# The router product of two tiles at once in three fp32r passes, in the output projection of an encoder layer

## The reference

```python
o = concat([rms_norm(o_a, gqa_out_norm_g), rms_norm(o_b, mla_out_norm_g)])   # heads' outputs, 1024 wide
h = h + o @ w_out                                                            # 1024 x 1024
u = rms_norm(h, norm_ffn_g)
lg = u @ w_rg + b_rg          # 4 groups
le = u @ w_re + b_re          # 32 experts
# the best group, and the best two of its 8 experts, then silu(x @ w_gate) * (x @ w_up) @ w_down
```

## Time and profile before

| what | value |
|---|---|
| median of 3 runs | 3897.84 us (3897.72 to 3899.2) |
| the profiled execution | 3894.24 us, its span 3892.3 us |
| mean granted clock of TensorE | 0.961 |
| the output projection in the trace | 2650.0 to 3033.0 us |
| in it, 2790 to 2990 us | PE busy 200.0, DVE 88.1, ACT 71.2 us |
| router products (L1688) | 384 passes, 192 products, 24 tiles |

### The profile page before, as it was taken

The page is one execution under the profiler, slowest core; times in us unless marked ns, Lnnn a source line. Parts: engine busy times, 40 slices in busy tenths (PEclk is TensorE's granted clock), DMA queues, the critical chain, the costliest instruction groups (busy, mean ns, idle before and its releaser), DMA issues. The chain is left out here.

```text
span 3892.3 us, 53957 instructions
## 1 busy us (share of the span) xinstructions
PE 3599.2 (92%) x17079; PEld 2878.0 (74%) x17079; DVE 2776.8 (71%) x4984; ACT 2341.2 (60%) x4266; POOL 1221.9 (31%) x1105
## 2 busy tenths in 40 slices
PE   7999969999999999999999999998999389999991
PEld 7999946666766676788888888876888367777770
DVE  5666668888988898889888988864444655555553
ACT  4444406777777777777777777785333055555554
POOL 0000001011110111488888888891000023333320
PEclk9999969999999999999999999998999799999995
DMA  5465681332133213320332133003433088888877
GB/s 178 164 228 174 199 197 63 65 65 44 27 63 65 44 27 65 63 55 16 65 64 44 27 64 65 7 8 114 146 135 124 23 275 261 269 261 258 257 210 281
DMA packets 315271, 462.88 MB, mean 119 GB/s; under 512 B 120641, under 2 KB 251997, under 8 KB 303869
## 3 DMA queue, kind: packets, MB, share of 16 engines
q1 hardware_dynamic: 256468, 368.47, 32.3%
q0 software_dynamic: 19152, 69.74, 7.0%
q10 hardware_dynamic: 39456, 22.29, 1.9%
HBM read 313.38 MB, written 147.54 MB: 118 GB/s over the span
## 5 line engine op out<-in xcount | busy, mean ns | idle before, releaser
L997 POOL TENSOR_TENSOR b_p_lo<-b_prob,b_p_hi 128x512 fp32r<-128x512 f32 x704 | 916.9, 1313 | 782.5 <-ACT b_prob L1041 778.1
L1040 ACT ACTIVATE b_p_hi<-b_psS 128x512 fp32r<-128x512 f32 (+1 forms) x1376 | 824.4, 599 | 531.1 <-PE b_psS L1232 512.8
L1232 PE MATMUL b_psS<-b_q,b_k 96*128 96x512 f32 (+3 forms) x3440 | 1067.6, 408 | 25.3 <-DMA b_q<-b_nmxT 23.5
L1041 ACT ACTIVATE b_prob<-b_psS 128x512 f32<-128x512 f32 (+1 forms) x1376 | 818.2, 595 | 0.0
L1232 PEld LDWEIGHTS b_psS<-b_q,b_k 96*128 96x128 f32 (+3 forms) x3440 | 599.8, 184 | 189.4 <-DMA b_q<-b_nmxT 26.4
L1142 DVE TENSOR_REDUCE b_mx_s<-b_psM 128x1 f32<-128x412 f32 (+1 forms) x1228 | 679.4, 580 | 68.6 <-PE b_psM L1283 58.2
L1283 PE MATMUL b_psM<-b_k,b_q 96*128 96x412 f32 (+7 forms) x1596 | 558.4, 355 | 29.5 <-DMA b_q<-QGL 21.8
L1273 PE MATMUL b_psO<-b_p_lo,b_v 128*65 128x512 f32 (+1 forms) x1280 | 508.3, 397 | 0.4 <-POOL b_p_lo L997 0.4
L1110 DVE TENSOR_TENSOR b_p_lo<-b_prob,b_p_hi 128x512 fp32r<-128x512 f32 x576 | 418.8, 733 | 66.0 <-ACT b_prob L1041 58.1
L1125 DVE TENSOR_TENSOR b_acc<-b_acc,b_prob 128x512 f32<-128x512 f32 (+1 forms) x592 | 409.3, 691 | 45.6 <-ACT b_prob L1041 29.6
L1283 PEld LDWEIGHTS b_psM<-b_k,b_q 96*128 96x128 f32 (+1 forms) x1596 | 305.0, 191 | 139.0 <-DVE b_mx_s L1142 32.6
(11 more groups left out here) (256 smaller groups left out, 5758.4 us busy)
## 6 DMA issues: line engine op xcount, KB each, us to landing
e_w_gu<-w_gate SPq DMA_DIRECT2D x34, 1024.0 KB, 6.2
e_w_gu<-w_up SPq DMA_DIRECT2D x34, 1024.0 KB, 12.4
e_w_dn<-w_down SPq DMA_DIRECT2D x34, 1024.0 KB, 14.0
a_x_raw<-xallT SPq DMA_DIRECT2D x25, 512.0 KB, 5.1
a_x<-xall SPq DMA_DIRECT2D x25, 512.0 KB, 4.2
c_o<-O SPq DMA_DIRECT2D x24, 512.0 KB, 4.9
c_x<-xall SPq DMA_DIRECT2D x24, 512.0 KB, 3.2
H<-c_h SPq DMA_DIRECT2D x24, 512.0 KB, 2.6
```

Source lines behind the costliest of these rows:

```text
L997: nc.gpsimd.tensor_tensor(p_lo[:, slot, :], prob[:, slot, :], p_hi[:, slot, :].bitcast(F32), ALU.subtract).then_inc(lo_ready, 1)
L1040: nc.scalar.activation(p_hi[0:kn, slot, :], psS[0:kn, j % 2, :], ACT.Exp)
L1041: nc.scalar.activation(prob[0:kn, slot, :], psS[0:kn, j % 2, :], ACT.Exp).then_inc(p_ready, 1)
L1232: m = nc.tensor.matmul(psS[0:kn, j % 2, :], kk[s][0:r, k], qq[s][0:r, q], start=n == 0, stop=n == len(passes) - 1)
```

## The change

The router product is made for two tiles at a time and with fp32r operands. `w_rr` holds the two parts of `w_r` side by side, 36 columns of the rounded weights and 36 of the rest; ACT and DVE make it once at the start. `uT` becomes `uT_hi` and `uT_lo`, each of two tiles: ACT rounds `psU` (`uT_round`), and DVE subtracts (`uT_rest`) where it had copied. `route(j)` multiplies `uT_hi` by all 72 columns and `uT_lo` by the first 36, 16 products of 256 columns, into 72 rows of `psR`. `lg_out(j)` adds the bias (0 in the second 36 rows) for both tiles. `l_turn(j)` multiplies by `fold`, two unit matrices one above the other, so that the rows are turned and added at once. Both stand in the odd tile only, l_turn before its y product and route behind it. y, the loads and the stores stay as they are.

```diff
--- before.py
+++ after.py
@@ -1394,7 +1394,9 @@
         w_hi = sb("w_hi", [P, KC, D], F32R)
         w_lo = sb("w_lo", [P, KC, D], F32R)
         w_r = sb("w_r", [P, KC, NR])
-        b_r = sb("b_r", [NR, 1])
+        w_rr = sb("w_rr", [P, KC, 2 * NR], F32R)
+        fold = sb("fold", [P, NR])
+        b_r = sb("b_r", [2 * NR, 1])
         g_ffn = sb("g_ffn", [P, D])
         eps = sb("eps", [P, 1])
         o = sb("o", [P, 2, D])
@@ -1412,13 +1414,14 @@
         hstd = sb("hstd", [P, 2])
         hr = sb("hr", [P, 2])
         u2 = sb("u2", [P, 2, D])
-        uT = sb("uT", [P, KC, P])
-        lg = sb("lg", [P, P])
+        uT_hi = sb("uT_hi", [P, KC, 2 * P], F32R)
+        uT_lo = sb("uT_lo", [P, KC, 2 * P], F32R)
+        lg = sb("lg", [P, 2 * P])
 
         psA = ps("psA", [P, 2, 512])
         psY = ps("psY", [P, 2, 512])
         psU = ps("psU", [P, 2, 512])
-        psR = ps("psR", [NR, 512])
+        psR = ps("psR", [2 * NR, 512])
         psL = ps("psL", [P, 512])
 
         small_loaded = sem("small_loaded")
@@ -1429,7 +1432,8 @@
         ostd_ready, orr_ready, os_ready = sem("ostd_ready"), sem("orr_ready"), sem("os_ready")
         oT_psum, oT_ready, hi_ready, lo_ready = sem("oT_psum"), sem("oT_ready"), sem("hi_ready"), sem("lo_ready")
         y_psum, h2_ready, hstd_ready = sem("y_psum"), sem("h2_ready"), sem("hstd_ready")
-        u2_ready, uT_psum, uT_ready = sem("u2_ready"), sem("uT_psum"), sem("uT_ready")
+        u2_ready, uT_psum, uT_rounded, uT_ready = sem("u2_ready"), sem("uT_psum"), sem("uT_rounded"), sem("uT_ready")
+        w_r_rounded, w_r_ready = sem("w_r_rounded"), sem("w_r_ready")
         r_psum, lg_ready, l_psum, l_ready = sem("r_psum"), sem("lg_ready"), sem("l_psum"), sem("l_ready")
         h_stored = [sem("h_stored0"), sem("h_stored1")]
 
@@ -1526,6 +1530,11 @@
                 nc.scalar.activation(hstd[:, s:s + 1], hss[:, s:s + 1], ACT.Sqrt, scale=1.0 / D,
                                      bias=eps[:, 0:1]).then_inc(hstd_ready, 1)
 
+            def uT_round(T, s):
+                act.wait_ge(uT_psum, T + 1)
+                nc.scalar.activation(uT_hi[:, :, s * P:s * P + P], psU[:, :, :].rearrange("p b (c n) -> p (b c) n", n=P),
+                                     ACT.Copy).then_inc(uT_rounded, 1)
+
             def w_round(c):
                 nc.scalar.activation(w_hi[:, c, :], w_raw[:, c, :], ACT.Copy).then_inc(w_hi_ready, 1)
 
@@ -1538,10 +1547,14 @@
             oT_rounded(0, 0)
             for c in range(2, KC):
                 w_round(c)
+            act.wait_ge(small_loaded, 16 * 3)
+            nc.scalar.activation(w_rr[:, :, 0:NR], w_r[:, :, :], ACT.Copy).then_inc(w_r_rounded, 1)
 
             def body(T, j, s):
                 if at_least(T, 1):
                     h_stats(T - 1, 1 - s)
+                if at_least(T, 2):
+                    uT_round(T - 2, s)
                 if below(T, N - 1):
                     oT_rounded(T + 1, 1 - s)
                 if below(T, N - 2):
@@ -1549,6 +1562,8 @@
 
             over_tiles(act, body)
             h_stats(N - 1, 1)
+            uT_round(N - 2, 0)
+            uT_round(N - 1, 1)
 
         @block.vector
         def _(dve):
@@ -1584,17 +1599,19 @@
                 nc.vector.scalar_tensor_tensor(u2[:, s, :], h2[:, s, :], hr[:, s:s + 1], g_ffn[:, :],
                                                ALU.mult, ALU.mult).then_inc(u2_ready, 1)
 
-            def uT_out(T):
-                dve.wait_ge(uT_psum, T + 1)
-                nc.vector.tensor_copy(uT[:, :, :], psU[:, :, :].rearrange("p b (c n) -> p (b c) n", n=P)).then_inc(uT_ready, 1)
-
-            def lg_out(T):
-                dve.wait_ge(r_psum, T + 1)
-                nc.vector.tensor_scalar(lg[0:NR, :], psR[:, 0:P], b_r[:, 0:1], None, ALU.add).then_inc(lg_ready, 1)
-
-            def l_out(T):
-                dve.wait_ge(l_psum, T + 1)
-                nc.vector.tensor_copy(logits[:, bass.ds(T * NR, NR)], psL[:, 0:NR]).then_inc(l_ready, 1)
+            def uT_rest(T, s):
+                dve.wait_ge(uT_rounded, T + 1)
+                part = slice(s * P, s * P + P)
+                nc.vector.tensor_tensor(uT_lo[:, :, part], psU[:, :, :].rearrange("p b (c n) -> p (b c) n", n=P),
+                                        uT_hi[:, :, part].bitcast(F32), ALU.subtract).then_inc(uT_ready, 1)
+
+            def lg_out(j):
+                dve.wait_ge(r_psum, j + 1)
+                nc.vector.tensor_scalar(lg[0:2 * NR, :], psR[:, 0:2 * P], b_r[:, 0:1], None, ALU.add).then_inc(lg_ready, 1)
+
+            def l_out(j):
+                dve.wait_ge(l_psum, j + 1)
+                nc.vector.tensor_copy(logits[:, bass.ds(j * 2 * NR, 2 * NR)], psL[:, 0:2 * NR]).then_inc(l_ready, 1)
 
             def w_rest(c):
                 dve.wait_ge(w_hi_ready, c + 1)
@@ -1613,12 +1630,16 @@
             oT_rest(0, 0)
             for c in range(2, KC):
                 w_rest(c)
+            nc.vector.tensor_tensor(fold[:, :], ident[:, 0:NR], ident[:, NR:2 * NR], ALU.add)
+            dve.wait_ge(w_r_rounded, 1)
+            nc.vector.tensor_tensor(w_rr[:, :, NR:2 * NR], w_r[:, :, :], w_rr[:, :, 0:NR].bitcast(F32), ALU.subtract)
+            dve.drain().then_inc(w_r_ready, 1)
 
             def body(T, j, s):
                 if at_least(T, 1):
                     h_out(T - 1, j - 1 if s == 0 else j, 1 - s)
                 if at_least(T, 2):
-                    uT_out(T - 2)
+                    uT_rest(T - 2, s)
                 if below(T, N - 1):
                     oT_out(T + 1)
                 if at_least(T, 1):
@@ -1627,23 +1648,21 @@
                     oT_rest(T + 1, 1 - s)
                 if below(T, N - 2):
                     o_recip(T + 2, s)
-                if at_least(T, 4):
-                    l_out(T - 4)
-                if at_least(T, 3):
-                    lg_out(T - 3)
+                if at_least(j, 2):
+                    if s == 0:
+                        lg_out(j - 2)
+                    else:
+                        l_out(j - 2)
 
             over_tiles(dve, body)
             h_out(N - 1, N // 2 - 1, 1)
-            uT_out(N - 2)
+            uT_rest(N - 2, 0)
             u_out(N - 1, 1)
-            l_out(N - 4)
-            lg_out(N - 3)
-            uT_out(N - 1)
-            l_out(N - 3)
-            lg_out(N - 2)
-            l_out(N - 2)
-            lg_out(N - 1)
-            l_out(N - 1)
+            lg_out(N // 2 - 2)
+            uT_rest(N - 1, 1)
+            l_out(N // 2 - 2)
+            lg_out(N // 2 - 1)
+            l_out(N // 2 - 1)
 
         @block.tensor
         def _(pe):
@@ -1678,46 +1697,46 @@
                     i = nc.tensor.transpose(psU[:, c // 4, (c % 4) * P:(c % 4) * P + P], uv[:, c, :], ident[:, :])
                 i.then_inc(uT_psum, 1)
 
-            def route(T):
-                if isinstance(T, int) and T == 0:
-                    pe.wait_ge(small_loaded, 16 * 3)
-                pe.wait_ge(uT_ready, T + 1)
-                if at_least(T, 1):
-                    pe.wait_ge(lg_ready, T)
-                for c in range(KC):
-                    i = nc.tensor.matmul(psR[:, 0:P], w_r[:, c, :], uT[:, c, :], start=c == 0, stop=c == KC - 1)
-                i.then_inc(r_psum, 1)
-
-            def l_turn(T):
-                pe.wait_ge(lg_ready, T + 1)
-                if at_least(T, 1):
-                    pe.wait_ge(l_ready, T)
-                nc.tensor.transpose(psL[:, 0:P], lg[:, :], ident[:, :]).then_inc(l_psum, 1)
+            def route(j):
+                if isinstance(j, int) and j == 0:
+                    pe.wait_ge(w_r_ready, 1)
+                pe.wait_ge(uT_ready, 2 * j + 2)
+                if at_least(j, 1):
+                    pe.wait_ge(lg_ready, j)
+                for c in range(KC - 1):
+                    nc.tensor.matmul(psR[:, 0:2 * P], w_rr[:, c, :], uT_hi[:, c, :], start=c == 0, stop=False)
+                    nc.tensor.matmul(psR[0:NR, 0:2 * P], w_rr[:, c, 0:NR], uT_lo[:, c, :], start=False, stop=False)
+                nc.tensor.matmul(psR[0:NR, 0:2 * P], w_rr[:, KC - 1, 0:NR], uT_lo[:, KC - 1, :], start=False, stop=False)
+                nc.tensor.matmul(psR[:, 0:2 * P], w_rr[:, KC - 1, :], uT_hi[:, KC - 1, :], start=False, stop=True).then_inc(r_psum, 1)
+
+            def l_turn(j):
+                pe.wait_ge(lg_ready, j + 1)
+                if at_least(j, 1):
+                    pe.wait_ge(l_ready, j)
+                for s in range(2):
+                    i = nc.tensor.matmul(psL[:, s * NR:s * NR + NR], lg[:, s * P:s * P + P], fold[:, :], start=True, stop=True)
+                i.then_inc(l_psum, 1)
 
             pe.wait_ge(mix_loaded, 16 * len(MIX_PARTS))
             o_turn(0, 0, first=True)
             o_turn(1, 1)
 
             def body(T, j, s):
-                if at_least(T, 4):
-                    l_turn(T - 4)
+                if s == 1 and at_least(j, 2):
+                    l_turn(j - 2)
                 y_of(T, s)
```

(16 more changed lines are left out.)

## The result

| what | before | after |
|---|---|---|
| median of 5 runs | 3898.94 us (3897.72 to 3902.82) | 3873.73 us (four of them 3865.32 to 3876.16) |
| after / before | | 0.9929, 95% interval 0.9916 to 0.9942 |
| the profiled execution | 3894.24 us, span 3892.3 | 3871.39 us, span 3869.5 |
| the output projection, first load to the first instruction of the routing | 383.3 us | 360.9 us |

The fifth run after took 5263.24 us at a mean granted clock of 0.628; the ratio leaves it out, the median counts it, and without it the median would be 3872.56.

What follows compares the result with a forecast made beforehand. TensorE's own instructions were taken to bound the output projection. Gains 17.5 + 2.2 + 1.35, less 0.75 and 0.3, made 20.0 us: 3877.8 us from the 3897.84 median, range 3874 to 3886.

Steps and rivals of the forecast that it cites:

- rival A: Output projection: the gain comes as worked out from what leaves TensorE's queue, 17 to 23 us; chance 73%.
- The u transposes: TensorE, each tile: transposes of u take 0.89 us after the change, against 0.99 behind the old router product.
- the o transposes: TensorE, each tile: transposes of o with the way to the next y take 0.81 us.
- the turn: TensorE, once per two tiles: two fp32 products turn the logits, 0.36 us plus 0.08 for the change of kind.
- the shorter tile at 22: Tile 22, without o transposes: TensorE waits for h, gap 1.7 us against 3.06 before, gain 1.35.
- rival C: A wait for h in even tiles, or the ScalarE/VectorE chain, takes up the gain; 3880 to 3898 us, chance 8%.
- rival B: Router product: weight loads show, 0.58 us a product, 6.3 us in all; gain 13.7, time 3884.1; chance 15%.
- the gap of 0.09: TensorE, ahead of the router product: a 0.09 us gap, assumed to remain once per two tiles.
- Sum of a steady pair of tiles: Loop, tiles 4 to 21: work between y products falls from 7.90 to 5.96 us a pair, gaining 17.5 us.
- The start: VectorE ahead of tile 1: fold matrix, second part of w_r and a drain cost 0.75 us, between 0 and 1.2.
- The end: Last y to last logits: cost 0.3 us, from -1 to +2.5, the upper end if the granted clock falls.
- a gain of 23 for the stage's terms: Output projection: largest gain taken into the range, with passes of 0.111 us and no 0.09 gap; 3874.8 us.

Runs made afterwards that it cites:

- experiment 2: Kernel before, with the router product for two tiles at once but still in fp32, DVE's copy and two plain transposes; 3894.79 us, 0.9993.
- experiment 3: Changed kernel with the fp32r router product one tile at a time, over 128 columns, and one fold product per tile; 3877.2 us, 0.9951.
- experiment 6: Changed kernel with w_rr and fold allocated behind all other tensors of the stage; 3874.44 us, 0.9945.
- experiment 5: Kernel before with the changed kernel's tensor places reserved in SBUF but unused, no instruction different; 3895.64 us, 0.9992.
- experiment 8: Changed kernel with a small stage ahead: fp32r passes of 512 columns at 16 pairs of operand places; 228.9 to 234.3 ns a pass.
- experiment 9: Changed kernel with 96 bytes a partition reserved in the expert stage ahead of x, xT and hT; 3866.72 us, 0.9927.
- experiment 11: Changed kernel run again unchanged, beside a version with all edits on the same chip; 3871.2 us, 0.9932.
- experiment 1: Changed kernel run again unchanged; 3873.22 us, 0.9941.
- experiment 4: Changed kernel with fold and w_r's second part made in tile 1's turn, and the last u ahead of the previous tile's uT; 3870.44 us, 0.9931.
- experiment 7: Changed kernel with experiment 4's two moves and unread transposes filling TensorE's idle stretches behind the loop; 3867.22 us, 0.9924.

## Why the prediction was right, and where it was off

**The mechanism** was as forecast (rival A). TensorE's queue was the time of the stage, and what left it was gained. A 256-column fp32r pass takes 0.117 us, as worked out from the pitch per column of the 346- and 512-column passes. The u transposes (0.89), the o transposes (0.81 to the next y), the turn (0.37, and 0.08 more on the transposes ahead of it) and the shorter tile at 22 (1.42 gained, forecast 1.35) came out as their rows said. No wait took the gain: rival C's first place, h, ends 0.5 us early, and its second closes 11.2 us after y's end. Experiment 2 shows that the rate of fp32r is the change's core, and experiment 3 that rival B's price doesn't exist even at half the length. The passes of 0.117 and 0.063 us show nothing of the weight loads: by rival B's price, 0.58 us, the product would take 2.45 us instead of its 1.87. With y's pass as it was (experiment 6), the loop's gain is 21.9 against 21.05. The 0.85 more is about what the gap of 0.09 ahead of the router product comes to over the ten that stand in the loop (0.9); the sum also left out the turn behind tile 3 (0.11). The gap belongs to the fp32 product, as experiment 2 still has it (2802.56 to 2803.12 is 0.56, not 0.47).

**The step that failed**, and put the median 0.3 us below the range, is "Sum of a steady pair of tiles". It wrote the tile as 11.20 us of y plus what lies between, and let only the second part change. That y stays at 11.20 was assumed without a reason, and it did not: y became 0.2289 a pass, 4.1 us over the loop and 0.2 in tile 23, because the new tensors w_rr and fold push oT to another place in SBUF: with them allocated last it is 0.2333 (experiment 6), and with their bytes reserved in the old kernel 0.2291 (experiment 5). There was no term for that. The diff shows the allocation, and no row of the kernel before shows that a place costs or gives time; experiments 5, 6, 8 and 9 do. Without it the stage's gain would have been 18.1 us, and the time, by an estimate from 3873.73 + 4.3, 3878, inside the range. Why the distance of two operands sets the pitch stays open.

**The start** was mis-sized by the clock. From the first y product of tile 0 to that of tile 1 it was 13.54 us, and it is 14.69 in the first profile after, by its timeline:

```profile
2665.56 1.22 PE L1687 MATMUL c_psY<-c_w_hi,c_oT_hi 128*128 128x512 f32 x2 [0.31 <-DVE c_oT_lo L1582]
...
2680.25 0.71 PE L1687 MATMUL c_psY<-c_w_hi,c_oT_hi 128*128 128x512 f32 x2 [0.34 <-DVE c_h L1590]
```

DVE's three things take 0.19, 0.45 and a drain. What they cost is seen at the product for tile 1 behind them, first before and then after:

```profile
2670.64 1.23 DVE L1562 TENSOR_TENSOR c_oT<-c_psA,c_g_out 128x1024 f32<-128x1024 f32 x1
```

```profile
2672.97 1.22 DVE L1577 TENSOR_TENSOR c_oT<-c_psA,c_g_out 128x1024 f32<-128x1024 f32 x1 [0.17 <-issue]
```

Counted from the first y product (2663.79 before), it starts at 6.85 and 7.41: 0.56 later, where 0.75 was forecast. In the three profiles where y of tile 0 was done early (experiments 3, 6 and 11) y of tile 1 comes at 14.10, 0.56 later than before. In this profile, and in experiments 1, 4 and 9, h of tile 0 sets it instead, since y of tile 0 took longer: 0.2636 a pass here against 0.2380 before, as the clock rose later: here the granted clock is 0.50 from the first pass to 2669, 0.53 to 2670 and 1.00 from then on, before it is 0.50 to 2665, 0.87 to 2666 and 1.00 from then on. Experiment 1's 14.31 us, 0.77 more than before, is near the forecast by luck, with 0.2553 a pass. With the three things moved (experiment 7) it is 13.54, the old value.

**The end** was forecast at 0.3 with 2.5 as its bound "if the granted clock falls", and it is 2.34: the bound's case was the true one. At a granted clock of 1.00 the end would be some 17.17 - 2.64 = 14.5 us, an estimate from experiments 4 and 7, 0.3 less than before, so the sum of the pieces was right within 0.6. All profiles with this end (the change, experiments 1, 6, 8, 9 and 11, and 4 with its shorter one) show the fall, from 1.00 to 0.50, and so do experiments 2 and 3 with ends of their own (idle for 2.75 and 4.80 us). TensorE's longest wait there became 3.80 us, for u, where it had been 3.08; u comes later by the rounding and the subtraction, which I had counted in time, while the clock stood only in the bound.

**Luck** made the total closer than its parts: the loop was forecast 4.9 us too low and the two ends 2.8 too high.

**The rest** is the scatter of the measurement. The medians differ by 25.2 us (the ratio gives 27.7, 22.6 to 32.8), the stages by 22.4 and the two profiled executions by 22.9. The range's lower end took in a gain of 23 for the stage's terms, but neither the place of operands nor the scatter of two medians, of some us on each side.

## What to carry to other kernels

A change in allocation can be a change in time (a y pass of 0.2333 us became 0.2289): when a tensor is added, compare the pitch of the matmuls it doesn't touch, and where TensorE sets the time of a stage, try the distance of weights and moving operand (192 bytes modulo 256, by an estimate of the places, was best here, 228.9 ns a pass against 232.4 to 234.3). Where fp32 products bound a stage, three fp32r passes are worth trying: here they paid at 128 columns (0.9951, 0.063 us a pass) as at 256 (0.9929, 0.117 us a pass), and no weight load showed. At the end of the stage the products behind TensorE's longest idle stretch ran at a granted clock of 0.50, or fell to it within 0.6 us, in every profile that had one but the first, (in the change a router pass of 256 columns took 0.213 us there instead of 0.117), on the path that sets the end; look at the granted clock there, and count an operand that comes later twice, for its own delay and for the clock.

## What the hardware showed that was not expected

- The pitch of a 512-column fp32r pass depends on the distance of its operands in SBUF (by the estimate of experiment 8): 228.9 ns at 192 bytes modulo 256, 234.1 to 234.3 at 96, and 232.4 to 233.3 at the other distances tried (0 was not). Why it does so stays open; so does tile 1 of the first profile.
- A 128-column fp32r pass with 36 or 72 columns of new weights takes 0.063 us (experiment 3).
- Around the end of idle stretches of 2.75, 2.88, 3.80 and 4.80 us TensorE's granted clock fell from 1.00 to 0.50, between 1.4 us ahead of its first product (experiment 1) and 0.6 us behind that product's start (experiment 8). After 3.08 us TensorE came back at a granted clock of 1.00 in one profile and of 0.50 in another (experiment 5), with the same instructions. The length of the idle stretch alone does not decide it, and what does was not tried.
